# Moving projection and output-projection steps one step earlier, and two gain loads into the start of the residual stage, in a one-core hybrid attention layer

## The reference

```python
u = rmsnorm(h, g_attn)
qa, ka, va, logf, qb, kb, vb = project(u, w_in, b_forget)
oa = fox(qa, ka, va, logf)          # 8 heads x 64, causal, with a forget bias
ob = swa(qb, kb, vb, ...)           # 8 query heads, 2 kv heads, 128-row window, sinks
mixed = concatenate([rmsnorm(oa, g_out_a), rmsnorm(ob, g_out_b)])
h = h + mixed @ w_out
u = rmsnorm(h, g_ffn)
h = h + (silu(u @ w_gate) * (u @ w_up)) @ w_down
y = rmsnorm(h, g_final)
```

## Time and profile before

| | |
|---|---|
| time, median of 3 executions | 1483.46 us (1483.01 to 1485.03) |
| the profiled execution: time, span | 1485.03 us, 1483.1 us |
| PE busy | 1410.7 us, 95% |
| DVE, ACT, POOL busy | 39%, 32%, 14% |
| DMA | 97.64 MB, 66 GB/s on average |
| mean granted PE clock | 0.976 of full speed |

### The profile page before, as it was taken

How to read it: one execution, slowest core, us unless ns; L and a number is a source line. 1 busy time by engine, 2 the same in 40 slices (tenths; PEclk the granted TensorE clock), 3 DMA queues, 4 the chain that set the end, 5 groups by cost and what they waited for, 6 DMA issues and landing times.

```text
span 1483.1 us, 22599 instructions
## 1 busy us (share of the span) xinstructions
PE 1410.7 (95%) x9041; PEld 1302.7 (88%) x9041; DVE 579.8 (39%) x1378; ACT 481.2 (32%) x1049; POOL 212.7 (14%) x317
## 2 busy tenths in 40 slices
PE   5989989899999989999999999999999999999996
PEld 3878878678788767788999999999999999999995
DVE  6235553323232333364324243333333342525155
ACT  6335553554545454264211202121111212121103
POOL 2125452253534223000000000000000000000000
PEclk8999999998999989999999999999999999999998
DMA  7611113311212045333311111111111202020003
GB/s 195 112 41 48 32 48 99 106 59 41 76 55 73 15 154 176 131 100 90 89 54 44 43 43 43 44 43 44 43 47 39 72 15 72 17 84 26 4 1 117
DMA packets 110255, 97.64 MB, mean 66 GB/s; under 512 B 15936, under 2 KB 96928, under 8 KB 109640
## 3 DMA queue, kind: packets, MB, share of 16 engines
q1 hardware_dynamic: 110152, 96.20, 22.1%
HBM read 77.07 MB, written 19.21 MB: 65 GB/s over the span
## 4 chain that ended last, share of the span: by engine, by line
PE 89%; DVE 4%; ACT 2%; DMA 2%; issue 2%; POOL 0%; SPq 0%; DVEq 0%; ACTq 0%
PE ps L573 27%; PE ps L574 26%; PE ps L575 26%; PE ps L775 3%; PE ps L915 1%; DVE ps L1582 1%; PE ps L743 1%; PE ps L705 1%; PE ps L787 1%; DMA out<-raw 1%; PE ps L652 1%; PE ps L587 1%; DVE sp_w L1594 1%; DMA cb<-c_scratch 1%; PE ps L846 0%
## 5 line engine op out<-in xcount | busy, mean ns | idle before, releaser
L1812 DVE TENSOR_TENSOR outs<-outs,ps 128x384 f32<-128x384 f32 (+1 forms) x264 | 134.5, 510 | 108.7 <-PE ps L575 108.7
L1797 DVE TENSOR_TENSOR gu<-ps,sg 128x384 f32<-128x384 f32 (+1 forms) x66 | 34.6, 524 | 237.9 <-PE ps L575 237.9
L1964 POOL TENSOR_TENSOR pl_x<-sp_x,ph_x 128x512 fp32r<-128x512 f32 (+5 forms) x120 | 101.9, 862 | 176.8 <-ACT sp_x L1217 175.2
L1396 ACT ACTIVATE h_hi<-gu 128x384 fp32r<-128x384 f32 (+1 forms) x66 | 32.9, 498 | 222.4 <-DVE gu L1797 222.4
L1216 ACT ACTIVATE ph_x<-ps,negc 128x512 fp32r<-128x512 f32 (+5 forms) x120 | 63.0, 525 | 87.3 <-PE ps L787 87.3
L1390 ACT ACTIVATE sg<-ps 128x384 f32<-128x384 f32 (+1 forms) x66 | 30.4, 464 | 171.7 <-PE ps L575 171.6
L573 PE MATMUL ps<-f_hi,ff0hi 128*128 128x384 f32 (+1 forms) x264 | 85.7, 325 | 0.0
L573 PE MATMUL ps<-f_hi,ff1hi 128*128 128x384 f32 (+1 forms) x264 | 85.6, 324 | 0.0
L573 PE MATMUL ps<-f_hi,ff2hi 128*128 128x384 f32 (+1 forms) x264 | 85.6, 324 | 0.0
L573 PE MATMUL ps<-f_hi,ff3hi 128*128 128x384 f32 (+1 forms) x264 | 85.6, 324 | 0.0
L574 PE MATMUL ps<-f_lo,ff0hi 128*128 128x384 f32 (+1 forms) x264 | 85.3, 323 | 0.0
(11 more groups left out here) (311 smaller groups left out, 3809.4 us busy)
## 6 DMA issues: line engine op xcount, KB each, us to landing
raw<-in_w_gate SPq DMA_DIRECT2D x22, 512.0 KB, 4.7
raw<-in_w_up SPq DMA_DIRECT2D x22, 512.0 KB, 4.8
raw<-in_w_down SPq DMA_DIRECT2D x22, 512.0 KB, 4.0
raw<-in_w_in SPq DMA_DIRECT2D x14, 512.0 KB, 4.0
cb<-c_scratch SPq DMA_DIRECT2D x4, 1312.0 KB, 7.1
xt<-in_x_prompt SPq DMA_DIRECT2D x8, 512.0 KB, 4.2
out<-outb SPq DMA_DIRECT2D x16, 256.0 KB, 2.4
ob<-o_scratch SPq DMA_DIRECT2D x16, 256.0 KB, 3.0
```

Of the source, the lines that this page charges most:

```text
L1396: act.activation(h_hi[par][:, f, c0:c0 + n], gu[(f + c) % 2][:, 0:n], ACT.Copy).then_inc(S["g_hi"], 1)
L1797: dve.tensor_tensor(gu[(f + c) % 2][:, 0:n], bank(3 + c, n), sg[c][:, 0:n], ALU.mult)\
L1812: add = dve.tensor_tensor(y, y, bank(6 + o % 2, whole * P).rearrange("p (t m) -> p t m", t=whole), ALU.add)
L1964: pool.tensor_tensor(pl_x[at][0:rows, 0:n], sp_x[at][0:rows, 0:n], ph_x[at][0:rows, 0:n].bitcast(F32), ALU.subtract).then_inc(S["x_pl"], 1)
```

## The change

Numbers of the schedule: the input projections of pairs 1 and 2 (steps 15 to 44) now have the same row of counts, and end in step 44, where 6 were left for step 45 before. The output projection begins in step 47 and not 48, with 4 steps and not 5 in each of the first six. The output weights are split one step earlier, as are the last pair's "fv" tasks and the turning of window tiles. In SP's queue, the load of `g_ffn` before stage W goes; `g_ffn` and `g_final` are both loaded in stage C, behind x1 of tile 1 and the first two FFN weights (which move ahead of x1 of tile 2). They swap halves of `gains`. The read-back of outputs of tiles 4 to 7 goes behind the loop.

```diff
-for _i, _steps in enumerate(((5, 5, 5, 6, 6, 5, 4, 4, 4, 4, 4, 5, 5, 5, 5), (6, 6, 5, 5, 5, 5, 4, 4, 4, 4, 4, 4, 4, 4, 2),
-                             (6,)), 1):
+for _i in range(1, PAIRS - 1):
+    FILL_X.update((NFU * _i + _j, _n) for _j, _n in enumerate((5, 5, 5, 6, 6, 5, 4, 4, 4, 4, 4, 5, 5, 5, 5)))
...
-FILL_O = {v: 5 for v in range(NX - 12, NX)}
-FILL_O.update({NX: 6, NX + 1: 6})
+FILL_O = {v: 4 + (v >= NX - 7) for v in range(NX - 13, NX)}
+FILL_O.update({NX: 6, NX + 1: 7})
-OUT_AT = tuple(NX - NFU + n for n in (1, 1, 2, 2, 6, 7, 8, 9))
+OUT_AT = tuple(NX - NFU + n for n in (0, 0, 1, 1, 5, 6, 7, 8))
...
-    VALUES_AT += [(_i, NFU * _i - 2, 3, (0, 4)), (_i, NFU * _i + (_i == PAIRS - 1), 3, (4, 4)),
-                  (_i, NFU * _i + 1 + (_i == PAIRS - 1), 0, (8, 1))]
+    VALUES_AT += [(_i, NFU * _i - 2, 3, (0, 4)), (_i, NFU * _i, 3, (4, 4)), (_i, NFU * _i + 1, 0, (8, 1))]
...
-        if v > NX - NFU + 1:
-            rows_turned(("x", v, 3), min(v - (NX - NFU + 1), TILES + 1))
+        if v > NX - NFU:
+            rows_turned(("x", v, 3), min(v - (NX - NFU), TILES + 1))
...
-            sp_.dma_start(gains[:, 0:D], spread(g_ffn, D)).then_inc(S["gain_in"], 16)
...
-                if v == NX - NFU + 1:
+                if v == NX - NFU:
                     sp_.wait_ge(S["pr_pe"], 3 * NW)
                     load_x(0, xb[0], "xb_in0")
                     load_x(1, xb[1], "xb_in1")
-                if v == NX:
-                    sp_.wait_ge(S["x_pv"], 2 * NX)
-                    sp_.wait_ge(S["x_og"], 16 * (3 * PAIRS - 1))
-                    for t in range(4, 8):
-                        load_outputs(t)
...
+            sp_.wait_ge(S["x_pv"], 2 * NX)
+            sp_.wait_ge(S["x_og"], 16 * (3 * PAIRS - 1))
+            for t in range(4, 8):
+                load_outputs(t)
             sp_.wait_ge(S["x_og"], 16 * 3 * PAIRS)
             load_outputs(8)
...
-                if t == 2:
+                if t == 1:
                     load_w(0, w_gate_v[:, :, 0:P], SPLIT_OUT + 7)
                     load_w(1, w_up_v[:, :, 0:P], SPLIT_FFN)
+                    sp_.wait_ge(S["g_pe"], T_OF["amx", PAIRS - 1, 2] + 1)
+                    sp_.dma_start(gains[:, D:2 * D], spread(g_ffn, D)).then_inc(S["gain_in"], 16)
+                    sp_.dma_start(gains[:, 0:D], g_final.partition_broadcast(P)).then_inc(S["g_final_in"], 16)
...
-            sp_.wait_ge(S["g_pe"], T_OF["amx", PAIRS - 1, 2] + 1)
-            sp_.wait_ge(S["x_og"], 16 * 3 * PAIRS)
-            sp_.dma_start(gains[:, D:2 * D], g_final.partition_broadcast(P)).then_inc(S["g_final_in"], 16)
```

More of the change, by code:

```diff
@@ L125 @@
 FILL_X.update(enumerate((3, 2, 3, 2, 3, 3, 3, 3, 3, 2, 3, 2, 3, 2, 2)))
-for _i, _steps in enumerate(((5, 5, 5, 6, 6, 5, 4, 4, 4, 4, 4, 5, 5, 5, 5), (6, 6, 5, 5, 5, 5, 4, 4, 4, 4, 4, 4, 4, 4, 2),
-                             (6,)), 1):
-    FILL_X.update((NFU * _i + _j, _n) for _j, _n in enumerate(_steps))
-FILL_O = {v: 5 for v in range(NX - 12, NX)}
-FILL_O.update({NX: 6, NX + 1: 6})
+for _i in range(1, PAIRS - 1):
+    FILL_X.update((NFU * _i + _j, _n) for _j, _n in enumerate((5, 5, 5, 6, 6, 5, 4, 4, 4, 4, 4, 5, 5, 5, 5)))
+FILL_O = {v: 4 + (v >= NX - 7) for v in range(NX - 13, NX)}
+FILL_O.update({NX: 6, NX + 1: 7})
 OUT_K = (4, 5, 6, 7, 0, 1, 2, 3)
-OUT_AT = tuple(NX - NFU + n for n in (1, 1, 2, 2, 6, 7, 8, 9))
+OUT_AT = tuple(NX - NFU + n for n in (0, 0, 1, 1, 5, 6, 7, 8))
 SQ_AT = {v: tuple(range(2 * (v + 7), min(2 * (v + 7) + 2, TILES))) for v in range(-7, -2)}
@@ L1761, in residual_norm @@
                 dve.scalar_tensor_tensor(out=xn2[0:m], in0=xc[t % 2][0:m], scalar=ri2_col[0:m, one],
-                                         in1=gains[0:m, 0:D], op0=ALU.mult, op1=ALU.mult).then_inc(S["c_xn2"], 1)
+                                         in1=gains[0:m, D:2 * D], op0=ALU.mult, op1=ALU.mult).then_inc(S["c_xn2"], 1)
             def residual_columns(t):
@@ L1855, in _ @@
                 dve.scalar_tensor_tensor(out=y_out[t % 2][0:m], in0=ps[0:m, b:b + 2, :].rearrange("p b n -> p (b n)"),
-                                         scalar=ri_col[0:m, one], in1=gains[0:m, D:2 * D], op0=ALU.mult, op1=ALU.mult)\
+                                         scalar=ri_col[0:m, one], in1=gains[0:m, 0:D], op0=ALU.mult, op1=ALU.mult)\
                    .then_inc(S["e_y"], 1)
```

## The result

| | kernel before | changed kernel |
|---|---|---|
| median of 4 executions | 1483.24 us (1482.13 to 1485.03) | 1495.56 us (1493.66 to 1496.23) |
| the profiled execution: time, span | 1485.03, 1483.1 us | 1494.8, 1492.9 us |
| PE busy, mean granted clock | 1410.7 us, 0.976 | 1411.9 us, 0.977 |

The ratio is 1.008, with a 95% interval of 1.0062 to 1.0097: the change makes the kernel slower, by 12.3 us in the medians. The forecast was 1491.3 us, with a range of 1485.8 to 1495.5. The direction and the place were right, the amount was 4.3 us too small, and the measured median lies a hair above the range's upper end.

A forecast was written before the change was run, and what follows sets the result against it. PE was taken as the bound, busy for 95% of the span; 8.5 + 2.0 - 2.7 = +7.8 us on the median of 1483.46 gave 1491.3 us, with an 8-in-10 range of 1485.8 to 1495.5.

The forecast's parts named there:

- The wait for the gains: Start of stage C: DVE's first residual add waits for g_ffn, delaying PE's second out_product and everything behind: +8.5 us.
- The clock after it: Start of stage C: after about 9 us of idle, PE comes back at a lower clock: +2.0 us, bounds 0 to 4.
- The beginning of pair 3: Steps 45 to 48: first output step 3.5 us earlier, less work still undone, plus clock saved: -2.7 us.
- A: Rival, start of stage C: g_ffn lands at its unloaded 5.0 us, shift 3.6; 1486.1 us, chance 0.13.
- C: Rival: the begin of pair 3 becomes like pair 2's and gives back 11.8 us; 1482.2 us, chance 0.04.
- B: Rival: the begin of pair 3 gives nothing or costs, +1 in place of -2.7; 1495.0 us, chance 0.15.
- at nothing: Parts priced at no cost, among them the outputs of tiles 4 to 7 coming 6 us later, before they are needed.

The follow-up runs named there:

- e1: The kernel before with only the gain loads and SP's order of loads changed, step counts as before: 1494.38 us, ratio 1.0067.
- e3: The changed kernel with DVE's wait for the gains moved to just before the product that reads them: 1487.99 us, ratio 1.0036.
- e4: The changed kernel with the two FFN weights (1 MB) put back behind x1 of tile 2: 1489.97 us, ratio 1.0050.
- e5: The changed kernel with the output loads of tiles 4 to 7 put back into the last pass: 1491.48 us, ratio 1.0053.
- e6: The changed kernel with the load of g_ffn put first, ahead of the output loads and x1: 1487.99 us, ratio 1.0037.
- e8: The kernel before with the new schedule tables, but one output weight split in step 45 instead of two: 1478.21 us in its one run.
- e2: The kernel before with only the new schedule tables, all loads where they were: 1483.30 us, ratio 1.0000.
- e7: The changed kernel with the edits of e3 and e5 together: 1484.12 us, ratio 0.9998.
- e10: The changed kernel with both edits of e7, and one output weight split in step 45 instead of two: 1484.51 us, ratio 1.0004.

## Why the prediction was right, and where its sizes were off

**The wait for the gains (+8.5 forecast).** It is there, in the place and by the mechanism that was named: e1 and e3 show that it is DVE's early wait for the gains, e4 and e5 that the gains are late by the bytes queued in front. Its size by the trace is +9.17 us. The rate taken from the earlier trace rows was right: the changed kernel moved 296 GB/s over 10 us. From the last turn of stage X to the issue of the first output load 1.21 us pass (1.1 in the forecast), and from that issue to the add 14.48 (13.9). These 0.6 us more were not counted; what they consist of, the traces don't show. The Trainium skill, page "DMA: Bandwidth & Descriptors", section "Where 436 GB/s comes from", puts the limit of a core's HBM traffic at about 358 GB/s. By it, as an estimate, the shift would have been 6.1 us (the prediction has 6.2). The trace does not agree: it stayed at 296 with its DMA engines 97% busy, and the row was the better guide. Nor was 358 a limit here, for e4 moved 409 GB/s over 2 us (last section). I was also right that PE has nothing else to do, and that nothing is caught up afterwards.

**The clock after it (+2.0).** Undersized: 3.0 us in the changed kernel (2.1 in e1, 2.9 in e4, 2.9 in e6). The rows it was taken from the earlier trace rows lay behind idle times of 3.1 and 4.4 us, and covered 4 and 5 us with a mean clock of 0.58 and 0.53; here nearly 6 us of work ran at 0.50. The bounds of 0 to 4 held it.

**The beginning of pair 3 (-2.7).** The chain over ACT and DVE came out closely: the minima product at 519.43 (forecast 519.9), the window tile at 522.58 (522.9), the first output step at 527.99 (528.2), 3.5 us nearer to the mark before pair 3, as forecast. PE's wait in step 46 was 3.55 us, not 4.7: the product came 0.5 us sooner and PE's work in front of it ended 0.7 us later (515.9 instead of 515.2) than I had them. What arrived at the end of stage X is -2.03 us in the trace. With the old tables the stretch from the mark to the last turn is 112.99 us in before and 113.10 in e1. In the ten traces with the new tables it is 110.6 to 111.0 in seven, 109.4 in e8, 111.56 in e5 and 112.86 in e3; PE's mean clock there was 0.92 in e5 and 0.91 in e3, and 0.94 in the changed kernel. The times don't show the gain: e2's ratio is 1.0000, with 3 us to either side. So some 2 us in most traces are shown; in the median they are not.

**The sum.** By the terms the profiled execution was to take 1485.03 + 7.8 = 1492.8 us; it took 1494.8. The 2.0 us are 0.67 (wait), 0.9 (clock and the rest of stage C), 0.67 (pair 3), less 0.25 that the changed kernel gained before the mark, which is inside the scatter told in the last section. The other 2.3 us of the miss lie outside the terms: the profiled execution of before stood 1.6 us above its median, and I carried this over, while the changed kernel's stands 0.8 us below its own. What was off in the prediction is therefore the size of two terms, the wait and its clock, forecast at 10.5 together and 12.1 in the trace, and the reading of one execution as if it carried a fixed offset from the median.

**The rivals.** A (the gains land unhindered) fell with the trace: they took 9.0 us from issue to landing, against 5.0 before. C (pair 3 becomes like pair 2) fell: 8.0 us of idle are left between 500 and 535 us. B named 1495.0 us, nearest to the measured time, but its mechanism, a beginning of pair 3 that costs 1 us, is not in the trace; its time was nearly met by luck, since the stall was larger. What none of them had is that x1 itself would be late behind the outputs, which the gains hid (e3: 3.08 us of waiting on PE). I had counted these loads as bytes in front of the gains only, and under "at nothing" looked at when their data is needed and not at what they push back.

**Left open.** How much of the -2 us of the schedule half is real in the median. It would take an interval of under 1 us, and this kernel's executions scatter by more than that. For the same reason no time shows whether the late gains, waited for at their use, still cost the 2 us of the traces.

## What to carry to other kernels

When a load moves to the end of a queue, sum the bytes in front of it, divide by the rate that a row of the trace shows for such loads, and look at which instruction waits and who stands behind it: a semaphore taken some instructions before the data is read turned a late gain vector into 9 us of an idle PE, where waiting at the use leaves 1.4 us of it (e7). Then repeat the sum for every other load behind the moved ones, because removing the latest wait can show the next. Add the low clock that follows an idle of PE as a cost of its own, and keep in mind that splitting work off into a waiting engine's queue (here a weight split in front of the exponentials) can cost its full 1.2 us there, and that taking it away again can bring the next stage's first step forward by only 0 to 0.3 us. A shorter wait alone proves no gain: look at when the instruction starts, since a slower engine also waits less.

## What the runs showed of the hardware

**Queued loads can be priced by one mean rate.** From the issue of the first load of the row to the add that used the last, in the traces of stage C:

| what the add waited for | MB up to and with it | us |
|---|---|---|
| x1, e3 | 1.64 | 8.01 |
| x1, e6 | 2.16 | 8.95 |
| gains, e5 | 2.69 | 10.55 |
| gains, e4 | 2.69 | 11.02 |
| gains, changed kernel | 3.74 | 14.48 |
| gains, e1 | 3.74 | 14.62 |

A line through e4 and the changed kernel has 3.3 us per MB (303 GB/s) and 2.1 us at zero bytes; it gives 7.5, 9.2, 11.0 and 14.5, and misses no row by more than 0.5 us. Where the product waited for the gains and not the add, it took 14.90 us for 3.74 MB in e3, and 11.65 and 11.51 us for 2.69 MB in e7 and e10, 0.5 to 1.1 more than the same bytes in e4 and e5. The one rate is a mean over unlike stretches. In e4:

```profile
618.00:620.00 2.00, 1.61 (x10) 1.11 (x8) 0.00 (x0) 0.00 (x0) 0.00 (x0) 1.00 0.84 241
620.00:622.00 2.00, 0.00 (x0) 0.00 (x0) 0.00 (x0) 0.00 (x0) 0.00 (x0) 1.00 1.03 409
```

In e5, which has the FFN weights in its row, it was 404 GB/s from 621 to 623, 311 from 623 to 627 and 401 from 627 to 629. By their order in the queue the slower stretches fit the output loads (e4) and the weights (e5), and the fast ones x1 and the gains; that it is so is argued from the order and not shown.

**The issue behind the two FFN weights is slow.** SP needs 0.42 us for the gate weights, but 4.06 us for the one load of `g_ffn` in the changed kernel, 4.81 in e1 and 3.81 in e3, with 3.2 MB in front of it in the row. The amount in front is not what decides: in e4, e5, e7 and e10 it is 2.16 MB each time, and the issue took 0.42 us in e4, but 2.95, 3.30 and 3.03 in e5, e7 and e10. What sets e4 apart is that the two weights do not stand in front. In e6, where `g_ffn` goes first, the load behind the weights is that of `g_final`, and it took 3.42 us. The weights come in rows of 128 numbers (512 bytes) where the others have rows of 2 to 4 KB; whether that is the reason was not tested. SP's other work behind a slow issue waits as long.

**The same code takes different times before the change even begins.** The mark before pair 3 stood at 503.03 us in before and 499.32 in e1, whose code up to there differs by one load, and between 499.6 and 504.5 in the others with the new tables. It is PE's instructions that take longer, not its waits: up to the mark PE is busy for 452.9 us in before, 449.6 in e1 and 454.5 in e5, and idle for 50.1, 49.7 and 50.0 us. The mean clock up to there was 0.96, 0.97 and 0.96. This scatter of some 5 us is why one execution can't tell 3 us, and why e8's 1478.21 us in one execution became 1482.95 in twelve. The 34 executions of before beside e1 to e4 run from 1475.1 to 1490.6 us.
